# Page numbers, page sums and the copy of old window rows: three steps of a hybrid decoder's one-core kernel put elsewhere

## The reference, cut to what matters

```
for i in range(DEPTH):                     # 2 layers
    mix = ssd_mixer(...) if i % 2 == 0 else nsa(...)
    h = layer_norm(ALPHA * x + mix)
    h = layer_norm(ALPHA * h + moe(h))     # 16 experts, top 2, each 1024 x 512 (gate, up) and 512 x 1024 (down)
    x = h + sigmoid(h @ ple_gate[i]) * (p[i] @ ple_proj[i])

def nsa_sample(h, kv_pool, page_table, win_cache, ...):
    past_cmp = kv_pool[page_table, :, 0:2]           # 8 pages of 128 rows for each of 8 decoding tokens
    kc, vc = nsa_compress(past_cmp ...)              # per block of 64 rows: sum over rows of row * softmax(pos_w)
    ...
    new_win = concat(win_cache[:, 1:], new row)      # the old rows are an output, shifted by one
```

## Time and profile before

| | us |
|---|---|
| median of 3 runs | 1119.33 (1116.6 to 1121.22) |
| the profiled execution | 1118.43 |
| its span, first to last instruction | 1116.7 |
| TensorE busy (matmuls) | 1036.7, 93% of the span |
| VectorE, ScalarE, GpSimd busy | 494.3, 306.3, 167.8 |
| moved by DMA | 346.33 MB, mean 310 GB/s |

### The profile page before, as it was taken

The page is one execution under the profiler, slowest core; times in us unless marked ns, Lnnn a source line. Parts: engine busy times, 40 slices in busy tenths (PEclk is TensorE's granted clock), DMA queues, the critical chain, the costliest instruction groups (busy, mean ns, idle before and its releaser), DMA issues. The chain is left out here.

```text
span 1116.7 us, 15016 instructions
## 1 busy us (share of the span) xinstructions
PE 1036.7 (93%) x5267; PEld 639.4 (57%) x5267; DVE 494.3 (44%) x1473; ACT 306.3 (27%) x785; POOL 167.8 (15%) x163
## 2 busy tenths in 40 slices
PE   7999998699999999999896999788999999999987
PEld 5788776488763444444475885344775443444456
DVE  1759798582531111111276996672162111111136
ACT  3111688910321111111132104462051111111124
POOL 0000002420000000000142833553000000000023
PEclk9899999899989999999998998999999999999999
DMA  9645598569429999999774975976984999999974
GB/s 317 220 160 188 154 282 276 197 226 395 189 77 396 427 429 425 428 427 427 297 301 164 394 247 166 326 244 219 428 345 151 403 429 425 428 427 426 429 313 204
DMA packets 89537, 346.33 MB, mean 310 GB/s; under 512 B 14770, under 2 KB 52658, under 8 KB 72402
## 3 DMA queue, kind: packets, MB, share of 16 engines
q1 hardware_dynamic: 82202, 321.94, 74.3%
q10 hardware_dynamic: 5240, 16.03, 3.9%
q0 software_dynamic: 2016, 7.34, 1.7%
HBM read 330.61 MB, written 23.04 MB: 317 GB/s over the span
## 5 line engine op out<-in xcount | busy, mean ns | idle before, releaser
L1460 DVE TENSOR_TENSOR acc<-acc,mo 128x264 f32<-128x264 f32 x64 | 27.5, 429 | 239.0 <-PE mo L1209 238.3
L518 PE MATMUL ss<-xT,expert_ring 128*128 128x264 f32 x384 | 92.9, 404 | 7.1 <-DMA expert_ring<-in_ssd_w_in 7.1
L1199 PE MATMUL mo<-expert_ring,gates_and_hidden 128*64 128x512 f32 x384 | 85.0, 595 | 8.2 <-ACT gates_and_hidden L1306 8.2
L1177 PE MATMUL mh<-expert_ring,x_packed 128*64 128x512 f32 x384 | 91.6, 603 | 0.0
L1158 PE MATMUL mh<-expert_ring,x_packed 128*64 128x512 f32 x384 | 89.1, 618 | 0.4 <-DMA expert_ring<-in_moe_w_gate 0.2
L518 PEld LDWEIGHTS ss<-xT,expert_ring 128*128 128x128 f32 x384 | 75.8, 200 | 21.4 <-issue 7.8
L1709 PE MATMUL na<-xT,expert_ring 128*128 128x264 f32 (+1 forms) x336 | 77.3, 394 | 11.2 <-PEq L1012 11.2
L1347 POOL DMA_INDIRECT x_rows_packed<-x_rows,slot_token_int x14 | 13.5, 961 | 476.6 <-DVE slot_token_int L1428 256.7
L1709 PEld LDWEIGHTS na<-xT,expert_ring 128*128 128x128 f32 (+1 forms) x336 | 64.1, 191 | 24.3 <-issue 11.9
L1469 DVE TENSOR_TENSOR gates_and_hidden<-mh,silu_gate 128x512 f32<-128x512 f32 x16 | 11.1, 691 | 132.8 <-PE mh L1177 132.8
L530 PE MATMUL ss<-xT,expert_ring 128*128 128x264 f32 x256 | 62.9, 400 | 6.3 <-ACT expert_ring_b L409 6.3
(11 more groups left out here) (419 smaller groups left out, 1844.2 us busy)
## 6 DMA issues: line engine op xcount, KB each, us to landing
expert_ring<-in_moe_w_down SPq DMA_DIRECT2D x24, 2048.0 KB, 18.0
expert_ring<-in_moe_w_gate SPq DMA_DIRECT2D x24, 2048.0 KB, 19.0
expert_ring<-in_moe_w_up SPq DMA_DIRECT2D x20, 2048.0 KB, 21.0
expert_ring<-in_ssd_w_in SPq DMA_DIRECT2D x9, 2048.0 KB, 7.9
expert_ring<-in_cmp_pages SPq DMA_DIRECT2D x40, 256.0 KB, 5.5
expert_ring_b<-in_moe_w_gate SPq DMA_DIRECT2D x4, 2048.0 KB, 17.4
expert_ring_c<-in_moe_w_gate SPq DMA_DIRECT2D x4, 2048.0 KB, 21.9
expert_ring<-in_moe_w_up SPq DMA_DIRECT2D x8, 1024.0 KB, 7.3
```

Source lines behind the costliest of these rows:

```text
L518: last = mm(pt[m % 4][:, 0:T], wc[:, k, ((m - 1) % 4) * P:((m - 1) % 4 + 1) * P], xT[:, k, :], start=k == 0, stop=k == KD - 1)
L1177: last = mm(hb[1][s * CAP:(s + 1) * CAP, :], xg[:, k, s * CAP:(s + 1) * CAP], unit(6 * i + 2 + s)[:, k * FF:(k + 1) * FF], start=k == 0, s ...
L1199: last = mm(ob[2 + a][s * CAP:(s + 1) * CAP, :], ht[:, k, s * CAP:(s + 1) * CAP], unit(6 * i + 4 + s)[:, o:o + 512], start=k == 0, stop=k ...
L1460: V.tensor_tensor(acc[:, d, :], acc[:, d, :], sc_bank[d % 4][:, 0:T], ALU.add).then_inc(acc_ok, 1)
```

## The change

Three steps are moved; every computation and every transfer stays.

1. The copy of `win_old` is issued in `tail(0)`, right behind expert unit 0, and no longer in `tail(1)`.
2. The 16 page numbers are read in `tail(0)` behind the last unit's issue, ahead of the waits for the experts and of `overflow`; before, they were read behind them.
3. The four sums of batch 0 leave the evacuation loop of `tail(0)` and stand at the start of VectorE's part of the attention block. With them goes the count of `c_used`.

```diff
                         load_unit(sp, L, 3 * L, unit(3 * L))
+                        if L == 0:
+                            sp.dma_start(O["win_old"], I["cache_win"][:, 1:, :]).then_inc(win_out, 16)
                         sp.wait_ge(gu_half, L + 1)
...
                             load_unit(sp, L, n, unit(n))
-                        if L == 1:
-                            sp.dma_start(O["win_old"], I["cache_win"][:, 1:, :]).then_inc(win_out, 16)
+                        if L == 0:
+                            page = [page_number(sp, n) for n in range(2 * NPG)]
...
                         overflow(sp, over_load)
                         if L == 0:
-                            page = [page_number(sp, n) for n in range(2 * NPG)]
                             load_cmp(sp, 0, page)
...
                             if m >= 1:
                                 finish(m - 1)
-                            if L == 0 and 2 <= m < 6:
-                                i1 = cmp_sum(V, 0, m - 2)
-                                if m == 5:
-                                    i1.then_inc(c_used, 1)
...
+                    for a in range(4):
+                        i1 = cmp_sum(V, 0, a)
+                    i1.then_inc(c_used, 1)
                     V.memset(kcx[:], 0.0)
```

## The result

The changed kernel takes **1125.99 us** (median of 6 runs, 1123.72 to 1128.82), the kernel before 1118.59 in the runs beside it (6 runs, 1116.60 to 1121.22): a ratio of **1.0065, 95% interval 1.0047 to 1.0083**. It is slower by 0.65%. The forecast was 1118.0 with a range of 1111 to 1124.5, so it was wrong, and on the slow side. The profiled execution took 1127.16 us, span 1125.4, 8.7 us more than the span of before.

What follows compares the result with a forecast made beforehand. TensorE, busy 93% of the span, was taken as the limit, with the DMA engines equally full through layer 0's experts. Terms 6 + 1.8 + 0 - 7.6 + 0 - 0.6 + 0 = -0.4 gave 1118.0 us, range 1111 to 1124.5.

Steps and rivals of the forecast that it cites:

- Term 1: Layer 0 routing: the copy delays x_rows' stores and POOL's gather, so TensorE waits for pair 1's rows: +6 us (0 to 10.4).
- rival A: Layer 0 routing: an engine passes all 8 rows of a store at once, only weights are late: 1113.3 us, chance 0.23.
- Rival B: Layer 0 routing: the gather meets the full stream and needs 12.3 us, a wait of 10.4: 1122.9 us, chance 0.18.
- term 4: End of layer 0: earlier pages and sums moved out let the projection start sooner: -7.6 us (-4.5 to -8.2).
- term 2: Layer 0, after the wait for rows: TensorE runs at half clock for a while: +1.8 us (1.7 to 2.3, or 0).
- term 7: End of layer 1: the copy gone from there changes nothing: 0, down to -0.5 us.
- Term 3: Layer 0 experts: weights fall 3.9 us behind, hidden by TensorE's own lateness: 0, or +3.1 us without that lateness.
- Term 5: Attention start: VectorE's 4.5 us of added sums fit in its wait for batch 2: 0, up to +2.2 us.
- term 6: Attention start: TensorE's shorter pause costs less time at half clock: -0.6 us (-2.2 to 0).
- Rival C: Attention: page loads set its pace and the sums move onto its path, 4.5 us come back: 1122.5 us, chance 0.05.

Runs made afterwards that it cites:

- 1: The kernel before with only the win_old copy moved behind unit 0 of layer 0: 1132.89 us, ratio 1.0137.
- 5: The changed kernel with the copy's two outer dimensions swapped, so the same packets go to 16 engines: 1111.33 us, ratio 0.9947.
- 7: The changed kernel with the copy in two halves of 7 KB packets, still on 8 engines: 1121.85 us, ratio 1.0045.
- 8: The changed kernel with the copy issued on ACT's queue behind the stores of the rows: 1134.02 us, ratio 1.0140.
- 13: The changed kernel with the layer 0 copy on 16 engines and TensorE's sum-of-squares matmuls one gate group later: 1110.83 us, ratio 0.9924.
- 9: The changed kernel with the copy on 16 engines and batch 0's multiplies also moved to the attention's start: 1114.38 us, ratio 0.9965.
- 4: The kernel before with only the page numbers read ahead: 1114.98 us, ratio 0.9980.
- 14: The changed kernel with the copy on 16 engines but in layer 1, and TensorE's sum-of-squares matmuls one gate group later: 1110.28 us, ratio 0.9926.
- 11: The changed kernel with the old copy back in layer 1 and TensorE's sum-of-squares matmuls one gate group later: 1110.75 us, ratio 0.9941.
- 10: The changed kernel with the old copy back in layer 1 and batch 0's multiplies also moved to the attention's start: 1116.16 us, ratio 0.9989.
- 2: The changed kernel with the copy put back in layer 1, so page numbers and sums alone: 1112.83 us, ratio 0.9959.
- 12: The changed kernel with the copy in two halves of 32 KB packets, on 8 engines: 1118.09 us, ratio 1.0016.

## Why the prediction was wrong

**Term 1, +6 us for the gather: the mechanism was right, the size was off; it was 13.4.** Copy on 8 engines, one row behind each piece, gather behind the stores: kernels 1, 5, 7 and 8 bear out each link, and rival A (rows pass the copy) is refuted. The rule beside it (the Trainium skill, DMA: Bandwidth & Descriptors, section on queues, rings and completion order: an engine drains a packet of typically 9 to 17 descriptors before it switches) doesn't show here: for 4 KB rows against 65 KB pieces the trace has 30 against 28. Two numbers were short. The rows landed at 345.5 at the latest and not at 342.3; 1.3 us of this is that unit 0 was issued later (292.09 against 290.77), the rest is mine. And the gather took 12.0 us to land, not 7.7. This is the step that failed, the price of the gather: I had two rows, 4.6 us with an idle queue and 11.7 to 12.3 beside the full stream, and chose the value near the first, because the halves of units 8 and 9 are small. But units 10 and 11, issued at 343.55 in pieces of 16 KB, were ahead of the gather too, and the stretch into which I had moved it was full: 429 GB/s from 346 to 352. Rival B, with its 12.3 and a chance of 0.18, was what happened; its 10.4 us of wait were short only by the rows' landing. With it the sum had been 1122.9, still within the range; the rows' 3.2 us or term 4's 2.6 on top of it lead out. With the rows' 3.2 it is 1126.1, and that this is near the measured time is luck: the misses of the other terms, +2.6 in term 4 and +0.7 in the attention against -1.3 in term 2 (2.3 in the rival's sum) and -0.8 in term 7, nearly cancel.

**Term 2, half clock, +1.8: measured 1.0.** The clock did fall. From the first turn to the down matmuls it is 3.50 us in place of 2.21, so 1.3 were lost; TensorE waits 0.69 us of that stretch for ScalarE in both kernels, and half speed costs nothing in a wait. Another 0.3 came back at pair 7, whose gate matmuls follow on the down matmuls 0.3 us sooner than in the kernel before.

**Term 3, the weights, 0: right, for the reason given.** The condition holds in three of four: where terms 1 and 2 are gone the experts take 1.7 (5), 7.2 (7) and 4.0 us (13) more, but none in kernel 9; the 3.1 was never met. Nor is the lead smallest at the last down unit, 0.8 us: at the gates of pair 7 TensorE waits 0.36 and 0.50 us for weights in kernels 4 and 14, which have no copy in layer 0.

**Term 4, -7.6: measured -5.0.** Both moves gave what they were priced at, 3.2 and 4.8 us alone, against 3.7 and 4.5. The floor was wrong. I took TensorE's last gate matmul at its old place, "which it reaches without a wait", and gave 1 us for GpSimd's squares beside VectorE's multiplies. It was 1.7 by the wait (2.38 in place of 0.66) and some 1.6 more by the clock behind it, 3.3 in all: the last gate matmul ended 39.2 us behind the last down matmul, where it was 35.9 before. The Trainium skill (GPSIMD Engine Reference, section "1. Specifications") says that GpSimd shares its SBUF interfaces with VectorE and contends with VectorE instructions that have two SBUF inputs, as these multiplies have; the trace agrees, 6.26 us for 4.63 on one side and 1.60 for 0.74 on the other. Kernel 11, without the wait, reached 7.6.

**Term 5, sums in the attention, 0: right as far as can be seen.** 478.5 us against 478.4, with term 6's gain in it, so up to 0.7 was lost against the forecast, less than the 3 us by which this stretch varies. VectorE's wait for batch 2 is 4.09 us in place of 7.33. Rival C is out for the sums, and came true in kernels 9 and 10 for the multiplies.

**Term 6, the clock at the attention's start, -0.6: about right.** In the first 6 us the granted clock is 0.58 and 0.85 in place of 0.50 and 0.76: 3 x 0.08 + 3 x 0.09 = 0.5 us.

**Term 7, layer 1 without the copy, 0: measured -0.8**, outside its bound of -0.5. The copy was over before the last store of y was issued at 1113.5, as I had said (behind 1113.4 no packet of 8 KB or more is left). What I missed are the three stores before it: they stand on the copy's own queue and land 5.4, 7.3 and 6.3 us after their issues, with the copy gone 2.0, and the last one, behind them, 2.8 in place of 2.0.

Together: 13.4 + 1.0 - 5.0 + 0.1 - 0.8 = 8.7 us. The forecast was -0.4, a miss of 9.1: term 1 alone is +7.4 of it, term 4 +2.6, the attention +0.7; terms 2 and 7 took 1.6 back.

**Left open.** Why TensorE's clock falls behind the 2.4 us pause in the changed kernel and in kernels 5, 7 and 8, and not in 2, 4 and 12, with the same pause behind the same work of the tail. No kernel prices the gather by itself: that the full stream makes it 12.0 us is read from the earlier trace rows and the stretch's 429 GB/s. And why the stretch through the attention varies by 3 us (477.9 to 480.9, in kernel 8 482.2) between kernels that don't differ there: kernels 11 and 13, with the later squares, have 480.9 and 480.8, and kernel 14, with the same edit, 477.9.

## What to carry to other kernels

A long transfer put into an idle queue is not free if something short and urgent passes the same engines: each packet of the short one waited here for one long packet, so look at the packet's length and at the number of engines first, and shape the transfer (here two swapped dimensions were worth 14 us) before choosing its place. When a step is moved in time, take its price from the rows of the stretch in which it will run, not from those where it runs today; of two bounds, the likely one is that of the busier queue. A wait taken from one engine lets it run beside others that had been alone: ask which of them slow each other (here VectorE and GpSimd), and put a cheap consumer (here two matmuls) one step later rather than let it wait.

## What the runs showed of the hardware

- Two queues on the copy's DMA engines took turns packet by packet, 28 to 30 in 8 us, with packets of 65 KB and 4 KB. A gather of 128 rows landed after 4.6 us alone, 8.5 beside the copy's 7 KB packets, 12.0 beside 16 KB and 8 KB packets, and 30.3 beside 65 KB ones.
- A copy between DRAM tensors with an outer dimension of 8 ran on 8 engines, with 16 on 16, and with 73 on a single one, at 27 GB/s, some 300 us for 8 MB.
- Four VectorE multiplies of 128x1024 took 4.63 us alone, 6.26 beside GpSimd's adds, and 8.94 where GpSimd's own multiplies ran beside most of them.
- The same pause of 2.39 us of TensorE was followed by full clock in one trace (sixteen matmuls in 3.76 us) and by a fallen one in another (4.80 to 5.44).
